# The first half of an input projection by seven half-size products, and sixteen modulation pages at another place

## The reference

```
def layer_forward(x, c, ...):                       # for the prompt and for the samples
    mod = silu(c) @ w_ada_l + b_ada_l               # 6 x 1024 numbers for each condition
    sh1, sc1, gt1, sh2, sc2, gt2 = split(mod, 6)
    h = rms_norm(x, g_mix_l) * (1 + sc1) + sh1
    z = h @ w_in_l                                  # 1024 x 4096
    q, k, v, u, g = split(z, [512, 1024, 1536, 2048])
    q, k = rms_norm(q by 64, q_gain), rms_norm(k by 64, k_gain)
    o = diff_attention(q, k, v, cached k and v)
    y = pool_mix(u, last 15 rows)                   # trailing windows, then a linear map
    merged = sigmoid(g0) * (o' @ w_branch[:512]) + sigmoid(g1) * (y @ w_branch[512:])
    x = x + gt1 * (merged @ w_out_l)
    h2 = rms_norm(x, g_ffn_l) * (1 + sc2) + sh2
    f = swiglu(h2, ...) if layer % 2 == 0 else moe_swiglu(h2, ...)
    return x + gt2 * f, k, v, ...
```

## Time and profile before

| | |
|---|---|
| median of three runs | 1605.14 us |
| the profiled execution | 1605.13 us, span 1603.2 us, granted clock 0.998 |
| TensorE (PE) busy | 1565.8 us, 98% of the span |
| weight loads on TensorE (PEld) | 1003.9 us, 63% |
| VectorE (DVE) / ScalarE (ACT) busy | 541.9 us / 181.6 us |
| DMA | 535.30 MB, mean 334 GB/s |

### The profile page before, as it was taken

One profiled execution on the slowest core, in us unless ns is written; L12 is line 12 of the kernel. 1 busy time (PEld: TensorE's weight loads), 2 busy tenths in 40 slices (PEclk: granted clock), 3 DMA queues, 4 the chain that ended last, 5 costly groups with the idle time before them and its releaser, 6 DMA issues.

```text
span 1603.2 us, 37188 instructions
## 1 busy us (share of the span) xinstructions
PE 1565.8 (98%) x16734; PEld 1003.9 (63%) x16734; DVE 541.9 (34%) x1182; ACT 181.6 (11%) x486; POOL 69.6 (4%) x118
## 2 busy tenths in 40 slices
PE   7999999999999999999999999999999999999997
PEld 3777898999998878944444444444554555555554
DVE  4368378666554783741101100110011011101132
ACT  2102313111112032131000000000000000000000
POOL 1112400000000110010000000000000000000010
PEclk9999999999999999999999999999999999999999
DMA  9999869666359755569999999999999999999995
GB/s 361 364 386 369 281 219 329 229 223 215 128 174 311 245 165 171 171 237 383 418 418 404 418 418 403 419 418 404 419 402 417 417 398 418 410 406 417 408 378 183
DMA packets 174340, 535.30 MB, mean 334 GB/s; under 512 B 12535, under 2 KB 101413, under 8 KB 161378
## 3 DMA queue, kind: packets, MB, share of 16 engines
q1 hardware_dynamic: 158706, 497.20, 80.9%
q0 software_dynamic: 8768, 28.96, 5.2%
q10 hardware_dynamic: 6704, 6.72, 1.3%
HBM read 517.47 MB, written 15.82 MB: 333 GB/s over the span
## 4 chain that ended last, share of the span: by engine, by line
PE 85%; DMA 11%; DVE 3%; issue 1%; ACT 1%; SPq 0%; DVEq 0%
PE banks L1885 30%; PE banks L1560 14%; PE banks L1199 14%; PE banks L1906 14%; DMA ring<-in_w_exp_up 10%; PE banks L1470 2%; PE banks L1740 2%; PE banks L1231 1%; DVE inv L2504 1%; PE banks L1727 1%; PE banks L1578 1%; DMA ring<-in_w_ada 1%; PE banks L1651 0%; DMA ring<-in_w_exp_down 0%; ACT hT L893 0%
## 5 line engine op out<-in xcount | busy, mean ns | idle before, releaser
L1885 PE MATMUL banks<-ring,area 128*32 128x448 f32 x3072 | 302.6, 539 | 3.3 <-DMA ring<-in_w_exp_up 2.7
L1885 PE MATMUL banks<-ring,xT 128*32 128x448 f32 x3072 | 301.8, 539 | 3.1 <-DMA ring<-in_w_exp_up 3.1
L1560 PE MATMUL banks<-hT,ring 128*128 128x264 f32 x1024 | 239.6, 389 | 3.8 <-ACT hT L893 3.7
L576 DVE TENSOR_TENSOR area<-banks,area 128x448 f32<-128x448 f32 x48 | 46.4, 966 | 576.4 <-ACT area L1157 576.4
L1906 PE MATMUL banks<-area 128*32 128x256 f32 x3840 | 227.4, 379 | 1.4 <-issue 1.1
L1560 PEld LDWEIGHTS banks<-hT,ring 128*128 128x128 f32 x1024 | 193.1, 191 | 39.3 <-issue 6.8
L1885 PEld LDWEIGHTS banks<-ring,area 128*32 128x32 f32 x3072 | 109.8, 110 | 164.5 <-issue 157.4
L1885 PEld LDWEIGHTS banks<-ring,xT 128*32 128x32 f32 x3072 | 111.7, 110 | 160.8 <-issue 151.5
L1906 PEld LDWEIGHTS banks<-area 128*32 128x32 f32 x3840 | 138.8, 110 | 100.6 <-issue 44.2
L1157 ACT ACTIVATE area<-banks 128x448 f32<-128x448 f32 x48 | 26.1, 543 | 779.3 <-PE banks L1885 779.3
L1906 PE MATMUL banks<-ring,area 128*32 128x256 f32 x1536 | 89.4, 379 | 2.0 <-DMA ring<-in_w_exp_down 1.4
(11 more groups left out here) (362 smaller groups left out, 1252.7 us busy)
## 6 DMA issues: line engine op xcount, KB each, us to landing
ring<-in_w_exp_gate SPq DMA_DIRECT2D x128, 896.0 KB, 17.6
ring<-in_w_exp_up SPq DMA_DIRECT2D x128, 896.0 KB, 19.7
area<-in_w_exp_down SPq DMA_DIRECT2D x64, 1024.0 KB, 18.1
ring<-in_w_ada SPq DMA_DIRECT2D x96, 512.0 KB, 8.6
ring<-in_w_in SPq DMA_DIRECT2D x32, 1024.0 KB, 13.6
ring<-in_w_exp_down SPq DMA_DIRECT2D x32, 1024.0 KB
area<-in_w_exp_down SPq DMA_DIRECT2D x32, 512.0 KB
ring<-in_w_ff_gate SPq DMA_DIRECT2D x11, 1024.0 KB, 6.4
```

The costliest lines, as they stand in the source:

```text
L576: dve.tensor_tensor(F["act_tok"][:, t, :].rearrange("p (i n) -> p n i", i=BODY), bank[3 + t][:, 0:SLICE].rearrange("p (n i) -> p n i", i=B ...
L1560: mm = pe.matmul(bank[b][:, 0:T], w[:, c, :], hT[:, c, :], start=(c == 0), stop=(c == DC - 1))
L1885: mm = pe.matmul(bank[t + 3 * half][32 * g:32 * g + 32, 0:SLICE], tokens[:, t, 32 * r:32 * r + 32], w[half][:, SLICE * g:SLICE * (g + 1)], ...
```

## The change

**Seven products.** A unit `u` is a pair of chunks (0 to 7). Units 1 to 7 of layer 0 and 1 to 6 of layer 1 are computed by seven half-size products, the other three as before (`z_whole`). In a unit TensorE does products 1 and 2, then the last product of the unit before (`z_fourth`), then 6, 5, 7, 3. VectorE adds four sums of weight blocks in each unit (`sum_z`, 512 elements a partition) and four reads of 132 columns (`z11`, `z12`, `z22`, `z21`), and in each layer four sums of `hT` (`sum_h_z`); the whole-chunk copies go. ScalarE gets three copies of 132 columns in each unit, and in layer 0 the five copies of the bias tables that VectorE made. `past_scores(0)` and `(1)` stand behind the last unit.

**Modulation.** `later_ada` ends at page 31: the four pages of units 0 to 3 stay, 32 to 47 go, 8 of them ahead of the output projection, 8 in the dense feed-forward, two in each of pairs 2 to 5, where two pages of layer 1 stand already.

```diff
+Z_UNITS = 8
+Z_HALVED = (1, 2, 3, 4, 5, 6, 7), (1, 2, 3, 4, 5, 6)
         def later_ada(l, i):
-            return range(16 + 2 * (i - 1), min(16 + 2 * (i + 1), 48)) if l == 0 and i % 2 else range(0)
+            return range(16 + 2 * (i - 1), min(16 + 2 * (i + 1), 32)) if l == 0 and i % 2 else range(0)
+        def last_ada(i):
+            return range(36 + 2 * i, 38 + 2 * i) if 2 <= i <= 5 else range(0)
...
+                    for n in range(32, 40) if (kind, l, j) == ("out", 0, 0) else ():
+                        yield ada_page(0, n)
...
+                def z_six_five(u):
+                    done = z_unit(l, u)
+                    pe.wait_ge(s.w_summed, z_summed(l, u, 1))
+                    pe.wait_ge(s.one_kept, done + 1)
+                    pe.wait_ge(s.h_summed, 12 * l + 2)
+                    product(z_left(u), z_w(u, 1), z_h(1), False).then_inc(s.product_mm, 1)
+                    pe.wait_ge(s.c11_read, done + 1)
+                    product(z_right(u), z_w(u, 0), z_h(0), True).then_inc(s.product_mm, 1)
+                def z_seven_three(u):
+                    pe.wait_ge(s.w_summed, z_summed(l, u, 3))
+                    pe.wait_ge(s.two_kept, done + 1)
+                    product(z_left(u), [unit[u][:, c, P:2 * P] for c in range(4)], z_h(2), False).then_inc(s.product_mm, 1)
+                    pe.wait_ge(s.five_kept, done + 1)
+                    product(z_right(u), z_w(u, 2), [hT[:, 4 + c, HALF:T] for c in range(4)], False).then_inc(s.product_mm, 1)
+                def z_fourth(u):
+                    pe.wait_ge(s.c22_read, z_unit(l, u) + 1)
+                    product(z_left(u), [unit[u][:, 4 + c, P:2 * P] for c in range(4)], z_h(3), False).then_inc(s.pages_used, 2)
...
+                for u in range(Z_UNITS):                      # TensorE
+                    if u in Z_HALVED[l]:
+                        z_first(u)
+                        z_second(u)
+                        if u - 1 in Z_HALVED[l]:
+                            z_fourth(u - 1)
+                            z_ada(u - 1)
+                        z_six_five(u)
+                        z_seven_three(u)
...
+                for u in range(Z_UNITS):                      # VectorE
+                    halved, before_halved = u in Z_HALVED[l], u - 1 in Z_HALVED[l]
+                    if before_halved:
+                        z12(u - 1)
+                    if halved and l == 0:
+                        sum_z(u, 0)
+                        sum_z(u, 1)
+                    if halved:
+                        z11(u)
+                    if before_halved:
+                        z21(u - 1)
+                    if halved:
+                        sum_z(u, 2)
+                        sum_z(u, 3)
+                    if u == 0:
+                        sum_h_z(0)
...
+                    if 2 <= u < 6:
+                        norm_qk(2 * u - 4)
+                    if u == 6:
+                        read_sample_queries()
...
+                    if halved:
+                        z22(u)
+                    if l and u + 1 in Z_HALVED[l]:
+                        sum_z(u + 1, 0)
+                        sum_z(u + 1, 1)
+                    if 2 <= u < 6:
+                        norm_qk(2 * u - 3)
...
+                    if u == 5:
+                        early_mod()
...
+                past_scores(0)
+                past_scores(1)
...
+                if l == 0:                                    # TensorE
+                    for n in range(32, 40):
+                        modulation(0, n, 7)
                 out_projection(l)
```

More of the change, by code:

```diff
@@ new lines, in _, with z_first @@
+                unit = {}
+                def z_first(u):
+                    w, arrived, count = z_page(l, u)
+                    unit[u] = w
+                    pe.wait_ge(arrived, count)
+                    if u >= 2:
+                        pe.wait_ge(s.z_out, ZC * l + 2 * (u - 2) + 2)
+                    if l == 0 and u == 1:
+                        pe.wait_ge(s.bias_out, 2)
+                    for c in range(4):
+                        mm = pe.matmul(z_left(u), w[:, c, 0:P], hT[:, c, 0:HALF], start=(c == 0), stop=(c == 3), skip_group_check=True)
+                    mm.then_inc(s.product_mm, 1)
@@ new lines, in z_second, with z_w, z_h @@
+                def z_second(u):
+                    product(z_right(u), [unit[u][:, 4 + c, 0:P] for c in range(4)], [hT[:, 4 + c, 0:HALF] for c in range(4)],
+                            True).then_inc(s.product_mm, 1)
+                def z_w(u, k):
+                    return [zw_sum[:, u % 2, k, c, :] for c in range(4)]
+                def z_h(k):
+                    return [zh_sum[:, k, c, :] for c in range(4)]
+                def z_six_five(u):
[6 more added lines that the diff above has]
+                    product(z_right(u), z_w(u, 0), z_h(0), True).then_inc(s.product_mm, 1)
@@ new lines, in z_fourth, with z_ada, z_whole @@
+                def z_fourth(u):
+                    pe.wait_ge(s.c22_read, z_unit(l, u) + 1)
+                    pe.wait_ge(s.h_summed, 12 * l + 4)
+                    product(z_left(u), [unit[u][:, 4 + c, P:2 * P] for c in range(4)], z_h(3), False).then_inc(s.pages_used, 2)
+                def z_ada(u):
+                    for n in later_ada(l, 2 * u + 1):
+                        modulation(l, n, 0)
+                def z_whole(u):
+                    w, arrived, count = z_page(l, u)
+                    pe.wait_ge(arrived, count)
+                    if u >= 2:
+                        pe.wait_ge(s.z_out, ZC * l + 2 * (u - 2) + 2)
+                    for i, b in ((0, Z_LEFT[u % 2]), (1, Z_RIGHT[u % 2])):
+                        for c in range(DC):
+                            if u == 0 and i == 0:
+                                pe.wait_ge(s.h_ready, 2 * DC * l + c + 1)
+                            mm = pe.matmul(bank[b][:, 0:T], w[:, c, i * P:(i + 1) * P], hT[:, c, :], start=(c == 0), stop=(c == DC - 1))
+                        mm.then_inc(s.pages_used, 1)
@@ new lines, in turn_state @@
+                def turn_state(n):
+                    if n == 0:
+                        pe.wait_ge(s.inputs_in, INPUTS)
+                        pe.wait_ge(s.rest_in, 16 * 3)
+                        pe.wait_ge(s.bias_out, H + 1)
+                    else:
+                        pe.wait_ge(s.state_out, n)
+                    for g in range(H):
+                        tr = pe.transpose(bank[1][:, g * 120:(g + 1) * 120], PRO["state_in"][:, n, g * P:(g + 1) * P],
+                                          ident[0:120, 0:120])
+                    tr.then_inc(s.state_mm, 1)
@@ new lines, in sum_qk, with turn_sample_queries @@
+                def sum_qk(j):
+                    if l == 0 and j == 0:
+                        pe.wait_ge(s.bias_out, H + 1)
+                    pe.wait_ge(s.qk_square, 8 * l + j + 1)
+                    if j >= 2:
+                        pe.wait_ge(s.qk_root, 8 * l + j - 1)
+                    pe.matmul(bank[6 + j % 2][:, 0:T], halves, sq[:, j, :], start=True, stop=True).then_inc(s.qk_sum_mm, 1)
+                def turn_sample_queries():
+                    pe.wait_ge(s.qk_ready, 8 * l + QC)
+                    pe.wait_ge(s.qk_root, 8 * l + 7)
+                    for h in range(H):
+                        t = pe.transpose(bank[6][0:NS, h * P:(h + 1) * P], ATT["q_n"][:, h, S:T], ident)
+                    t.then_inc(s.qs_mm, 1)
@@ new lines, in turn_sample_keys @@
+                def turn_sample_keys():
+                    pe.wait_ge(s.qk_ready, 8 * (l + 1))
+                    for h in range(H):
+                        t = pe.transpose(bank[7][0:NS, h * P:(h + 1) * P], ATT["kT"][:, h, S:T], ident)
+                    t.then_inc(s.qs_mm, 1)
+                for u in range(Z_UNITS):
+                    if u in Z_HALVED[l]:
+                        z_first(u)
[5 more added lines that the diff above has]
+                        z_seven_three(u)
+                    else:
+                        if u - 1 in Z_HALVED[l]:
+                            z_fourth(u - 1)
+                            z_ada(u - 1)
+                        z_whole(u)
+                        z_ada(u)
+                    if l == 0 and u in STATE_AT:
+                        turn_state(STATE_AT.index(u))
+                    if 1 <= u < 5:
+                        sum_qk(2 * u - 2)
+                        sum_qk(2 * u - 1)
+                    if u == 5:
+                        turn_sample_queries()
+                    if u == 6:
+                        turn_sample_keys()
@@ new lines, in z12, with z22 @@
+                def z12(u):
+                    dve.wait_ge(s.product_mm, z_finished(l, 3, u))
+                    dve.wait_ge(s.two_kept, z_unit(l, u) + 1)
+                    dve.tensor_tensor(z_chunk(2 * u)[:, HALF:T], z_right(u), z_kept2[:, u % 2, :], ALU.add).then_inc(s.z_out, 1)
+                def z22(u):
```

(3 more changed lines are left out.)

340 lines of the change are left out of this document (195 added, 145 removed).

## The result

The changed kernel takes 1612.51 us (median of six, 1609.67 to 1614.6) against 1605.16 us before: ratio 1.0043, 95% interval 1.0033 to 1.0053. It is slower by 0.43%, where 0.14% faster was forecast, and lies outside the range. Its profiled execution took 1614.60 us with a span of 1612.9, 9.7 over the span before; at 2.1 us over the median it is the longest of the six, so its waits are rather large ones. The kernel before, measured again beside each group of experiments, had medians of 1605.28 to 1606.02; single traces lie up to 3.6 us off the median of their kernel.

The account below looks back on a forecast made before the run. TensorE's own work bounds both projection stages, with DMA saturated in layer 0's. From 1605.13: -10.7 - 0.6 + 3.8 + (2.3 + 0.5 + 1.0) + 0.6 + 0.9 = -2.2, giving 1602.9 us; range 1597.5 to 1608.3.

Parts of the forecast that it names:

- Products: Halved units on TensorE: a half-size product costs 0.90 us, and 13 pairs save 0.82 each, 10.7 us less.
- VectorE's length: A unit from 2 to 5 takes VectorE 7.9 us against TensorE's 7.2, longer by 0.7 where no modulation stands.
- layer 1: Layer 1's units: TensorE stalls 0.65 us in each of units 3 to 5 and 1.85 before unit 6, together 3.8.
- fourth rival: Every VectorE operation counts with its shown length, a unit 8.6 us, both layers losing more: 1608.1 us; chance 0.12.
- the second: Rival: VectorE's chain hides and TensorE stays the bound, leaving only page wait and some restarts: 1595.1 us; chance 0.14.
- Behind the units: Later past scores after the units: 0.5 us of stall at L1578 in layer 0, 0.1 in layer 1, together 0.6.
- Modulation: The 16 moved pages cost 7.5 us in either place, nothing net; fewer places behind pages save 0.6 us.
- the forecast's last sign: If the gap between the layers' feed-forward parts changes by over 1 us, the moved pages were not free.
- third rival: Queries' way through DRAM delays the first score; decides if landing is over 12 us behind the copy: 1608.1; chance 0.16.
- Pages: Layer 0, unit 3: TensorE wants its pages at 61.0, they land at 62.0, so it waits 1.0 us.

Follow-up runs that it names:

- e5: Changed kernel with VectorE's copy of the new rows (read_new) one score earlier, ahead of past_scores(6): 1607.67 us.
- e1: Changed kernel with no unit halved in either layer, the new list order and moved modulation pages kept: 1612.81 us.
- e13: Changed kernel with no unit halved and the modulation pages at their old places, only the new list order kept: 1608.17 us.
- e10: Changed kernel with two modulation pages a unit in layer 0, both layers' modulation reads moved, read_new one score earlier, queries a unit earlier, past_scores(0) earlier: 1599.51 us.
- e2: Changed kernel with only layer 0's units 1 to 7 halved, none of layer 1, pages moved: 1612.95 us.
- e7: Changed kernel with VectorE's modulation read in unit 4 of layer 0 and unit 1 of layer 1 instead of unit 5: 1612.29 us.
- e8: Changed kernel with unread products added in layer 0, four ahead of unit 2 and two ahead of unit 6's product 6: 1611.02 us.
- e12: e10 with no unit halved in either layer: 1606.07 us.
- e4: Changed kernel with all 13 units halved but the modulation pages at their old places: 1607.78 us.

## Why the prediction was wrong, step by step

*Products, VectorE's length, layer 1: right.* In the changed kernel, TensorE in unit 3 of layer 1:

```profile
512.96 1.06 PE L1708 MATMUL banks<-hT,ring 128*128 128x132 f32 x8
513.86 1.06 PE L1273 MATMUL banks<-hT,ring 128*128 128x132 f32 x8
...
517.98 1.17 PE L1273 MATMUL banks<-area,ring 128*128 128x132 f32 x8 [0.23 <-DVE ring L2488]
...
520.78 1.06 PE L1708 MATMUL banks<-hT,ring 128*128 128x132 f32 x8
```

A product costs 0.90 (512.96 to 513.86). The unit takes 7.82 (512.96 to 520.78), VectorE's 7.9 and not TensorE's 7.2. The bracket shows 0.23, not 0.65: the product ahead of it is drawn longer, and only the period tells the stall of 0.6. Units 4 and 5 are alike, and in unit 6 the brackets come to 1.55 (forecast 1.85). The layer's first half got 0.8 shorter (forecast 1.1), and mended the halves give 1.2 there. Unit 6 of layer 0 waited 2.3 and unit 7 0.5, as forecast. The fourth rival (lengths of 0.69, a unit of 8.6) is out; so is the second.

*"Behind the units", 0.6: the step that failed first.* In the changed kernel VectorE starts its scores 0.4 behind chunk 16's start at 111.50 (forecast 0.3), but the third one 8.8 behind it instead of 7.1:

```profile
111.91 0.68 DVE L2556 TENSOR_TENSOR area<-area 128x512 f32<-128x512 f32 x1
...
120.29 0.69 DVE L2556 TENSOR_TENSOR area<-area 128x512 f32<-128x512 f32 x1 [1.58 <-DMA area<-in_cache_k]
...
137.20 0.67 DVE L2630 COPY area<-banks 23x512 f32<-23x512 f32 x1
```

and GpSimd's queue, which loads the cached keys into four slots in turn, issues the first of its reloads here (the bracket is the queue's own idle time before, not the load):

```profile
113.25 0.54 POOL L844 DMA_DIRECT2D area<-in_cache_k  x1 [7.05 <-DVE area L2556]
```

The sum gave back 1.9 us of waits for keys "if DMA is lighter, as it should be". They did not go: 2.1 in layer 0, which is 1.5 of the 1.6 us that the sum missed there, and 3.2 in layer 1 where there had been 1.2. A slot is asked for when a score has read it (113.25) and its page is there at 120.29, 7.0 later, while four pages of scores last 5.8 (111.91 to 117.71). That is the delay of one load, and it begins with the first score, which the change put behind the units; that the loads came a little sooner than before (5.1 us in the median from issue to landing instead of 5.9) did not help. In layer 1 the sum looked at L1699 and passed over `score(1)`: there `read_new` ended 5.5 us later against chunk 16 than before (26.8 behind it instead of 21.3), where 2.7 was forecast and 2.9 was slack. `score(1)` waited 2.1 and 2.6 instead of 0.5 and 0.1; e5 took 4.8 us off by this place alone. By the fit of the Trainium skill (DMA: Bandwidth & Descriptors, "Anatomy of one DMA", 2.0 us and the bytes at 436 GB/s) a load of 256 KB would be 2.6 us by estimate; the trace's 3.4 to 6.9 in this full queue (12 loads of layer 0) decide.

*"Modulation", -0.6: failed most.* Measured is +4.6 us (e1 less e13). The price of a page was right: 7.5 forecast, 7.25 measured, and the stages that took the pages grew by it and no more (3.8 and 3.5), so the forecast's last sign, a gap changed by over 1 us, tells nothing of a loss there. Wrong was that the stage would be as much shorter. Its end is not TensorE's own: what is queued between the turned queries and the new rows keeps its length, and TensorE, 7.9 sooner at the turn, had 4.9 of it taken at the branch. The third rival named that way (queries, DRAM, first score) and judged it by its landing only. In the changed kernel the queries landed 11.7 us behind the end of their copy, just under the 12 named, and 0.4 us ahead of the first score, so as it was put it is out; but in e1 the score did wait for them (0.87), and that e10's edit took the wait at `score(1)` away shows the chain as a whole to be the limit.

*"Pages", 1.0: wrong unit and size.* I had weighed unit 3 alone; TensorE waited at unit 2, 3.8 us in the profiled execution (2.6, 2.7 and 0.2 in e5, e2 and e7). The product starts between 53.7 and 54.1 in all four, once the pages are there; how long TensorE has waited by then varies with its own start, 7.4 to 10.0 us for the first 32 matmuls. Counting from 52.59 on hid the first two units, where TensorE before was kept busy to 55.01; now it was ready at 50.3.

*The clock: no term at all.* In the profiled execution the slow stretches cost about 3.1 behind unit 2's wait (54.08 to 61.72 is 7.64 for three products and four pages, 2.7 + 1.87), 1.8 in unit 6 (3.55 for two products instead of 1.80) and 1.8 behind `score(1)` (5.51 for 3.72). Waits were costed at their length alone. e8 gives what filling two of them brings.

*Halves together.* Forecast -2.2 with all side costs but the order and pages; measured -0.3, within the noise nothing. I put the missing 2 us down to unit 2's pages and the clock in layer 0, which no run separates; that stays open. Mended, the halves bring 6.6 (e12 less e10).

## What to carry to other kernels

Time taken from a stretch is gained only if nothing that ends behind it is a chain of its own: draw the chain with the longest way through other engines and DRAM (here queries, DRAM, seven scores, new rows) and ask where it starts, before pricing what TensorE saves. A slot that is loaded again costs a whole load's delay from the moment its reader frees it (7.0 us here), so ask when its first reader comes. And a new wait of TensorE of two us or more can cost more than its length: where the slow clock followed, it took 1.8 to 3.1 us on top in the changed kernel.

## What the runs showed of the hardware

The clock does not answer to a wait's length alone. Behind 2.33 and 2.13 us of idle time it fell (0.52, 0.69), behind 2.56 in layer 1 it did not (3.83 for 16 matmuls of 264 columns). In the sixteen traces, behind the first 32 matmuls of each layer's stage and up to its branch products, it fell behind 7 of 13 waits between 2.0 and 2.9 us, and behind all 7 longer ones (3.1 to 4.2). And the first 32 of layer 0's stage, each time behind the same 2.04 us, took 7.36 in the changed kernel and in e10,

```profile
34.96 7.36 PE L1763 MATMUL banks<-hT,ring 128*128 128x264 f32 x32 [2.04 <-ACT hT L941]
```

8.9 to 9.1 before and in ten of the experiments, and 10.0 in e4, e7 and e12. These instructions are the same in all; the difference of up to 2.7 us is one between single executions and may be part of the spread of 5 us within one kernel. What decides it stays open.
